# Half of the modulation vectors of a two-block network: from TensorE matmuls to VectorE multiply-and-sum, on one core

## What is computed

```python
for i in range(DEPTH):                      # two layers
    mod = silu(c) @ ada_w[i] + ada_b[i]     # c: 1024, ada_w[i]: 1024 x 6144
    sh1, sc1, g1, sh2, sc2, g2 = split(mod, 6)
    mod_c = silu(c_ctx) @ ada_w[i] + ada_b[i]   # the same for the context
    h = rmsnorm(x) * (1 + sc1) + sh1        # and hc of ctx by mod_c
    y, yc = attention(h, hc) if i == 0 else ssm(h, hc)
    x = x + g1 * y
    x = x + g2 * swiglu(rmsnorm(x) * (1 + sc2) + sh2)
    ...                                     # ctx likewise, in layer 0
```

## Time and profile before

| | |
|---|---|
| time, median of 3 runs (lowest, highest) | 1482.14 us (1481.31, 1489.8) |
| the profiled execution: time, span | 1486.74 us, 1484.9 us |
| TensorE busy | 1441.1 us, 97% of the span |
| VectorE busy | 801.4 us, 54% |
| ScalarE busy | 628.9 us, 42% |
| GpSimd busy | 295.3 us, 20% |
| moved from and to device memory | 206.81 MB, mean 139 GB/s |
| mean granted TensorE clock | 0.988 |

### The profile page before, as it was taken

One profiled execution on the slowest core, in us unless ns is written; L12 is line 12 of the kernel. 1 busy time (PEld: TensorE's weight loads), 2 busy tenths in 40 slices (PEclk: granted clock), 3 DMA queues, 4 the chain that ended last, 5 costly groups with the idle time before them and its releaser, 6 DMA issues. The chain is left out here.

```text
span 1484.9 us, 22118 instructions
## 1 busy us (share of the span) xinstructions
PE 1441.1 (97%) x9039; PEld 1202.4 (81%) x9050; DVE 801.4 (54%) x1341; ACT 628.9 (42%) x1183; POOL 295.3 (20%) x217
## 2 busy tenths in 40 slices
PE   7999999999989999999999999999999999999997
PEld 6978888888755778888888887888998778888886
DVE  6775645465299363233222324864543876476674
ACT  4536444653378343221122223442443574364452
POOL 2002355350000012110021110444500121021121
PEclk9999999999999999999999999999999999999999
DMA  7643688553100252223232333232451253656551
GB/s 229 216 146 113 233 319 324 190 194 150 57 1 1 75 209 85 85 89 134 76 112 69 100 110 119 86 113 85 142 179 49 103 182 140 258 181 215 177 175 48
DMA packets 36124, 206.81 MB, mean 139 GB/s; under 512 B 4968, under 2 KB 9496, under 8 KB 14904
## 3 DMA queue, kind: packets, MB, share of 16 engines
q1 hardware_dynamic: 32832, 199.58, 37.3%
q10 hardware_dynamic: 2376, 3.04, 1.1%
q0 software_dynamic: 816, 2.78, 0.6%
HBM read 202.76 MB, written 2.62 MB: 138 GB/s over the span
## 5 line engine op out<-in xcount | busy, mean ns | idle before, releaser
L645 DVE TENSOR_TENSOR w_split<-ring,w_split 128x1024 fp32r<-128x1024 f32 (+1 forms) x140 | 193.0, 1381 | 326.3 <-ACT w_split L640 325.7
L640 ACT ACTIVATE w_split<-ring 128x1024 fp32r<-128x1024 f32 (+1 forms) x140 | 157.9, 1133 | 369.6 <-PE lin L2085 259.2
L2083 PE MATMUL lin<-hn_hi,w_split 128*128 128x512 f32 x440 | 172.8, 393 | 0.0
L2085 PE MATMUL lin<-hn_hi,w_split 128*128 128x512 f32 x440 | 171.3, 389 | 0.0
L2084 PE MATMUL lin<-hn_lo,w_split 128*128 128x512 f32 x400 | 155.7, 389 | 0.0
L2115 PE MATMUL lin<-hn_hi,w_split 128*128 128x512 f32 x328 | 114.0, 394 | 0.0
L587 POOL TENSOR_TENSOR hn<-hn 128x256 f32<-128x256 f32 (+1 forms) x36 | 44.4, 1234 | 334.7 <-ACT hn L737 334.3
L604 POOL CAST hid_split<-arena 128x512 fp32r<-128x512 f32 (+1 forms) x44 | 26.0, 592 | 407.0 <-DVE arena L1167 269.7
L2083 PEld LDWEIGHTS lin<-hn_hi,w_split 128*128 128x128 f32 x440 | 82.6, 188 | 18.2 <-issue 1.3
L2085 PEld LDWEIGHTS lin<-hn_hi,w_split 128*128 128x128 f32 x440 | 82.6, 188 | 17.4
L645 POOL TENSOR_TENSOR w_split_od<-ring,w_split_od 128x1024 fp32r<-128x1024 f32 x31 | 75.7, 2455 | 81.7 <-ACT w_split_od L640 81.6
(11 more groups left out here) (517 smaller groups left out, 3481.0 us busy)
## 6 DMA issues: line engine op xcount, KB each, us to landing
ring<-ada_in SPq DMA_DIRECT2D x48, 1024.0 KB, 5.1
ring<-ssm_in_in SPq DMA_DIRECT2D x24, 1024.0 KB, 4.8
ring<-od_in_in SPq DMA_DIRECT2D x12, 1024.0 KB, 5.3
ring<-ffn0a_in_in SPq DMA_DIRECT2D x11, 1024.0 KB, 4.8
ring<-ffn0b_in_in SPq DMA_DIRECT2D x11, 1024.0 KB, 4.8
ring<-ffn1a_in_in SPq DMA_DIRECT2D x11, 1024.0 KB, 4.9
ring<-ffn1b_in_in SPq DMA_DIRECT2D x11, 1024.0 KB, 4.8
ring<-ev_in_in SPq DMA_DIRECT2D x9, 1024.0 KB, 13.4
```

Source lines behind the costliest of these rows:

```text
L640: act.activation(parts[:, 0], w, ACT.Copy).then_inc(sig("w_high"), 1)
L645: dve.tensor_tensor(parts[:, 1], w, parts[:, 0].bitcast(F32), ALU.subtract).then_inc(sig("w_low"), 1)
L2083: mm(lin[0:m, tile % RING, 0:width], hi, x_hi, start=kt == 0, stop=False)
L2085: ins = mm(lin[0:m, tile % RING, 0:width], lo, x_hi, start=False, stop=kt == kts - 1)
```

## The change

24 of the 48 modulation blocks stay with TensorE (output tiles 0 to 39 and 88 to 95, groups 0 to 4 and a last one that is now number 5). The other 48 output tiles (40 to 87) are laid out the other way round, outputs on the partitions and the 1024 inputs along the row (`ada_rows`, 24 blocks of 1 MB, two tiles in each). VectorE multiplies such a tile with a row vector that stands on all partitions and sums along the row in the same instruction (`accum_out`), once for c and once for c_ctx: four instructions of 128 x 1024 a block, 96 in all, two after each of the units 4 to 51 (of 60) of the first feed forward. The row vectors come by a new load of 1 MB on GpSimd's queue (`c_rows`), which waits until the last tile of `w_o` has been read, and ScalarE applies silu to them (128 x 2048). `STREAM` carries the row blocks between the weights of the first feed forward.

```diff
-    *[(name, n, 2 * KT * P) for _ in range(6) for name, n in (("od_in", 1), ("ada", 2))],
-    *[(name, 1, 2 * KT * P) for _ in range(3) for name in ("od_in", "ada")], ("ada", 1, 2 * KT * P),
-    ("od_out", 4, 2 * KT * P),
+    *[(name, n, 2 * KT * P) for _ in range(4) for name, n in (("od_in", 1), ("ada", 2))],
+    ("od_in", 5, 2 * KT * P), ("od_out", 4, 2 * KT * P),
...
-    ("ada", 2, 2 * KT * P), ("ffn0a_in", 2, 2 * KT * P), ("ada", 2, 2 * KT * P), ("ffn0a_in", FH - 2, 2 * KT * P),
-    ("ffn0a_out", KT, FH * P), ("ffn0b_in", FH, 2 * KT * P), ("ffn0b_out", KT, FH * P),
+    ("ada", 2, 2 * KT * P), ("ffn0a_in", 4, 2 * KT * P),
+    *[(name, 1, 2 * KT * P) for _ in range(7) for name in ("ada_rows", "ffn0a_in")],
+    *[part for _ in range(4) for part in (("ada_rows", 1, 2 * KT * P), ("ffn0a_out", 2, FH * P))],
+    *[(name, 1, 2 * KT * P) for _ in range(11) for name in ("ada_rows", "ffn0b_in")],
+    *[part for _ in range(2) for part in (("ada_rows", 1, 2 * KT * P), ("ffn0b_out", 2, FH * P))], ("ffn0b_out", 4, FH * P),
...
+            taken(pool, "lin", lin_of["w_o"] + KT - 1)
+            pool.dma_start(c_rows, t["c_rows"].unsqueeze(0).to_broadcast([P, 2, D])).then_inc(sig("c_rows_in"), 16)
             sum_squares(pool, own, 3, 2 * L)
...
+            act.wait_ge(sig("c_rows_in"), 16)
+            act.activation(c_rows, c_rows, ACT.Silu).then_inc(sig("silu_rows"), 1)
             ffn_scalar(act, 0, 2 * L)
...
-            for stage, u, later in ffn_units(n):
+            for v, (stage, u, later) in enumerate(ffn_units(n)):
                 tile = lin_of[stage] + u
                 if later is not None:
                     weights_lo(dve, *later)
-                if stage[-4:] == "a_in" and u == 8:
-                    modulations(dve, own, group, 1)
+                if n == 0 and 4 <= v < 4 + 2 * ROW_BLOCKS:
+                    modulation_rows(dve, own, v - 4)
...
+        def modulation_rows(dve, own, m):
+
+            r, j = divmod(m, 2)
+            b, n = blocks_of["ada_rows"][r], ROW_TILES + m
+            if m == 0:
+                dve.wait_ge(sig("silu_rows"), 1)
+            if j == 0:
+                dve.wait_ge(w_in[b % RING], 16 * (b // RING + 1))
+            for s in range(2):
+                ins = dve.scalar_tensor_tensor(
+                    out=row_products, in0=ring[:, b % RING, j * D:(j + 1) * D], scalar=1.0, in1=c_rows[:, s],
+                    op0=ALU.mult, op1=ALU.mult, accum_out=mod_tiles[:, n, s:s + 1])
+                own.link(ins)
+            if j == 1:
+                dve.sem_inc(sig("ada_rows_used"), 1)
+            if m in (7, 2 * ROW_BLOCKS - 1):
+                tiles = slice(ROW_TILES if m == 7 else ROW_TILES + 8, n + 1)
+                own.link(dve.tensor_tensor(mod_tiles[:, tiles], mod_tiles[:, tiles], each(mod_bias[:, tiles], 2), ALU.add))
...
-                if 3 <= u_ < 16 or u_ == 17 or 20 <= u_ < 23:
+                if 3 <= u_ < 12:
                     ada(1)
...
-                if 5 <= n < 7:
-                    ada(1)
...
             for i in range(DT_ + 2):
-                if i in (5, 12, 16):
-                    ada_groups((5, 12, 16).index(i) + 8)
                 if i == DT_:
                     y_sums(0)
-                if i < 2 or 5 <= i < 9 or 12 <= i < 16:
-                    ada(1)
...
-                if 5 <= n < 7:
-                    ada(1)
```

More of the change, by code:

```diff
@@ L379, in program @@
         silu_g = mem.take(2, 2 * L)
+        row_products = mem.take(D)
+        c_rows = mem.take(2, D)
         mem = Memory(arena)
@@ L847, in od_weights @@
                     weights_hi(act, "qkv", m)
-            act_norm(act, 2, 2 * L, "od_out", (0, 0, 0), before=od_weights, later=6)
+            act_norm(act, 2, 2 * L, "od_out", (0, 0, 0), before=od_weights, later=4)
             def exps(i, j):
@@ L915, in first_weights @@
                 weights_hi(act, "ssm_in", 1)
-            act_norm(act, 4, 2 * L, "ffn0b_out", (1, 0, 2), first_weights, between=lambda: weights_hi(act, "ssm_in", 2))
+            act_norm(act, 4, 2 * L, "ffn0b_out", (1, 0, 2), first_weights, between=lambda: weights_hi(act, "ssm_in", 2),
+                     later=5)
             weights_hi(act, "ssm_in", 3)
@@ L1021, in next_weights @@
                         weights_hi(act, "ffn1a_in", m)
-            act_norm(act, 5, L, "ssm_out", (1, 3, 3), before=next_weights, later=11)
+            act_norm(act, 5, L, "ssm_out", (1, 3, 3), before=next_weights)
             ffn_scalar(act, 1, L)
@@ L2003, in _ @@
             q1_low(KT - 1)
-            modulations(dve, own, 0, 6)
+            modulations(dve, own, 0, 4)
             def query_weights(n):
@@ L2656, in feed_forward @@
                         split_linear(stage + "_in", KT, lambda kt: (hn_hi[:, kt, :], hn_lo[:, kt, :]), width,
-                                     later=later, norm=start)
+                                     norm=start)
                         split_linear(stage + "_out", FH, lambda kt: (hid_split[:, 0, kt, :], hid_split[:, 1, kt, :]),
@@ L2891, in layout @@
                           for n in range(2)])
-    o["ada"] = ada
+    o["ada"] = np.concatenate([ada[:20], ada[44:]])
+    rows = np.stack([i["ada_w_2"][n].T.reshape(48, P, D) for n in range(2)]).reshape(96, P, D)
+    rows = rows[ROW_TILES:ROW_TILES + 2 * ROW_BLOCKS].reshape(ROW_BLOCKS, 2, P, D)
+    o["ada_rows"] = rows.transpose(0, 2, 1, 3).reshape(ROW_BLOCKS, P, 2 * D)
+    o["c_rows"] = np.stack([i["c_2"][0], i["c_ctx_2"]])
     o["gcol"] = columns(i["norm_g"])
```

59 lines of the change are left out of this document (31 added, 28 removed).

## The result

The changed kernel takes 1489.57 us (median of 20 runs, 1486.17 to 1492.86), the kernel before 1486.83 in the 20 runs beside it (1481.31 to 1489.8): a ratio of 1.0027, 95% interval [1.0017, 1.0037]. By this interval the change costs 2.5 to 5.5 us where 2.7 us of gain were forecast. The forecast of 1480 was tied to the 1482.14 of the three runs shown then; the larger set puts the kernel before 4.7 us higher, so 4.7 of the 9.6 us between 1480 and 1489.6 are this reference, and the rest is the error of the prediction. The kernel before varies with its clock: of 11 runs on one chip five took 1481.5 to 1482.9 us at a mean granted clock of 0.991, the other six 1487.0 to 1488.3 at 0.988. By the profiled executions the span grew from 1484.9 to 1490.1 us, and the mean granted clock fell from 0.988 to 0.977.

A forecast was written before the change was run, and what follows sets the result against it. TensorE was taken as the bound. 25.0 saved - 10.0 seams - 8.1 norm - 4.2 clock = 2.7 us faster than the profiled 1486.74, so 1484.0, or 1479.5 by the runs' median; predicted 1480, range 1466 to 1500.

The forecast's parts named there:

- TensorE's clock: Half-speed stretches behind new pauses: 1.7 us at each of two seams, 0.8 at the norm behind w_o, together 4.2 lost.
- the two blocks at the norm that follows fill waits of TensorE: nothing: At the norm behind ssm_out, taking out two blocks that fill TensorE's waits was to save nothing.
- TensorE saves 25.0 us: Blocks and groups removed: od_in 9.0, w_o 2.5, loop over heads 10.6, ssm_out 2.3, feed forwards 0.6 us.
- the wait for VectorE's shares: In the attention behind od_in, TensorE arrives earlier without the blocks and waits 1.7 us for VectorE.
- Row sum 1.3 us: Time of one summing VectorE instruction in the first feed forward; 96 of them 125 us, VectorE keeping pace up to 1.95 each.
- Seams 10.0 us: Between in- and out-product, TensorE waits for VectorE's last product: 4.9 and 5.1 us, bounds 3.4 and 16.
- the ring's lateness: At a seam, the third out-block loads only after unit 19's row sums, landing at 668.8, 4.3 us late.
- Norm behind `w_o` 8.1 us: The c_rows load ahead of GpSimd's six sums of squares makes TensorE wait 8.1 us longer, range 7.5 to 9.
- Rival A: First feed forward: VectorE becomes the pace from 1.95 us a row sum; at 2.3 us about 1523 us; chance 0.13.
- Rival B: Seams cost little, with the ring never late and the clock staying: 1469 to about 1466 us; chance 0.15.
- Rival C: ScalarE and VectorE pace the loop over heads, its 10.6 us saving shrinks to some 4: 1486 us; chance 0.12.

The follow-up runs named there:

- e3_both: Changed kernel with the c_rows load issued behind GpSimd's sums of squares and the row sums around the seams moved into out-units: 1464.50 us, ratio 0.9873 to before.
- e2_seam: Changed kernel with no row sums around the seams, their eight tiles' sums moved into the first half's out-units: 1477.33 us, ratio 0.9952 to before.
- e1_norm: Changed kernel with the c_rows load issued behind, not ahead of, GpSimd's sums of squares at the norm behind w_o: 1478.56 us, ratio 0.9957 to before.
- e6b_fill: Changed kernel with useless matmuls in TensorE's new pauses, 37 at the norm behind w_o and 16 at either seam: 1482.89 us, ratio 0.9984 to before.
- e10_load: Kernel before with only the c_rows load added ahead of GpSimd's sums of squares, all blocks staying with TensorE: 1493.90 us, ratio 1.0061 to before.
- e5_fill5: Changed kernel with load and seam row sums moved, plus ten useless matmuls at each of two places at the norm behind ssm_out: 1465.00 us, ratio 0.9871 to before.
- e4_none: Changed kernel without the row-block and c_rows loads, the silu and the 96 row sums: 1466.61 us, ratio 0.9873 to before.
- e7_path: Changed kernel without the row sums of units 18, 19, 48 and 49: 1481.39 us, ratio 0.9977 to before.
- e8_twice: Changed kernel with every row sum done twice, one behind the other: 1575.46 us, ratio 1.0605 to before.

## Why the prediction was wrong, step by step

The step that failed is **"TensorE's clock": "I count 1.7 for each of the two new pauses at the seams ... the longer pause may add 0.8. Together 4.2, bounds 0.8 and 6."** The mechanism was right, the size was not. I had taken the price of a pause from one place, the 1.88 us at 304.28 with its 3 us at 0.50, and used it for pauses of 4.6 and 9.7. Even for its own length that was one case of several: this pause is the same in all 14 executions (1.86 to 1.88 us), and 3.4 us at 0.50 follow it in five, 6.8 in two, none in seven. Windows behind it in the changed kernel, e3_both and e2_seam:

```profile
297.60:300.50 2.90, 2.90 (x14) 2.90 (x15) 0.79 (x3) 1.18 (x2) 0.04 (x1) 0.50 0.71 246
293.90:299.80 5.90, 5.90 (x27) 5.90 (x28) 0.81 (x3) 1.58 (x2) 2.39 (x1) 0.50 0.49 181
296.50:300.50 4.00, 4.00 (x33) 4.00 (x34) 0.89 (x4) 1.68 (x3) 1.81 (x1) 1.00 0.76 266
```

And at the norm behind `w_o` the kernel before is at 0.50 from 547.2 to 550.6; the 2.2 us of the earlier trace rows are only the part of it that was read.

Measured, the out-products are 7.5 and 7.9 us longer with pauses of 4.59 and 4.76, so 6.05 for the clock at the seams (3.4 predicted; 4.1 in e1_norm); filling the pauses gave 4.7 of these back with the hold left nearly as it was (e6b_fill). At the norm behind `w_o` it is 2.0 (0.8 predicted; e10_load has it alone). And one more place was counted at nothing: "the two blocks at the norm that follows fill waits of TensorE: nothing" is true of the waits, but without them the stretch at 0.50 behind that norm doubled from 3.4 to 6.8 us in the changed kernel, and fills there took it away (e5_fill5, in the trace alone). It costs 1.0: the second feed forward is 0.4 longer, though it lost a group of 0.6. Together some 9.1 against 4.2 and beyond the bound of 6: these 4.9 us are more than the 2.7 of the forecast, and turn its sign. The figure is that of the profiled executions; in a run of the median time it is some 2 us lower.

The Trainium skill (TensorE: Matmul & The Clock Gate, under Terms) puts the penalty at the throttled time by one less the ratio, here half of it. For the seams that gives 3.4 each by the stretch of 6.8; measured are 3.0, since TensorE was still waiting in a part of it. The halving was not what I missed, it was the length.

Point by point:

- **TensorE saves 25.0 us.** About 23.1: `od_in` 8.2 (9.0 predicted; the wait for VectorE's shares 1.55, 1.7 predicted), `w_o` 2.5 (2.5), loop over heads 10.2 (10.6), `ssm_out` 1.6 (2.3), groups 0.6 (0.6). The trace of e4_none agrees; its 18.9 us by time are this saving less what the clock took back. A second, smaller error, 1.9 us.
- **Row sum 1.3 us.** Right: 1.244 in the mean, one every 1.26 with the read-out (656.70 to 657.95 and 661.44 to 662.70 in the trace). The Trainium skill's halving (Vector Engine (DVE) Microarchitecture Reference, under Points that are easy to get wrong) is not borne out for this form, by which one would have taken some 2.3.
- **Seams 10.0 us.** Right: 9.35, by the very chain that was written down. The third out-block is issued at 664.02 at the end of unit 19's sums, has landed when ScalarE starts on it at 668.08 (668.8 predicted), the product comes at 677.82 and TensorE goes on at 680.58 (681.4 predicted). e7_path leaves 1.79 and 2.00 without the ring's lateness (1.7 predicted).
- **Norm behind `w_o` 8.1 us.** 9.0: the order is as predicted, but six sums take 8.85 and not 8.1, since one of them ran beside VectorE's work and took 2.13 us. The top of the range of 7.5 to 9 is just what came.
- **Rival A** did not come about; e8_twice shows its mechanism at twice the size; where between the two it sets in was not tried. **Rival B**, seams that cost little: no, they cost 15.4 us with the clock. **Rival C**, a loop over heads paced by others: no, 10.2 of 10.6 came.

The measured terms give 23.1 - 9.35 - 9.0 - 9.1 = -4.35, so 4.3 us slower; the profiled executions differ by 5.2. The rest lies at places that are not in this sum: 1.3 slower ahead of the norm behind `ev_out`, 1.4 faster in the attention, 0.8 slower behind the norm of `ffn0b_out` (6.8 us at 0.50 in place of 3.4) and 0.4 at the end. Stretches at 0.50 come and go also where no edit reaches: ahead of the norm behind `ev_out`, where all executions run the same code, they sum to between 0 and 6.8 us, and the stage lasts 170.6 to 174.5 us; in the attention the changed kernel had one fewer than the kernel before.

## What to carry to other kernels

Price a new pause of TensorE at its length plus the work behind it at half speed, and take the stretch from pauses of similar length, in more than one execution: here 4.6 to 4.9 us of waiting cost 6.2 to 7.9. Before work is handed to an idle engine, look at what the handing over puts into other queues: one DMA issue ahead of six sums cost 11 us here, and sixteen of 96 row sums beside a seam another 15, while the other eighty cost next to nothing; moving both turned +0.3% into -1.3%, and two smaller touches made it -1.7%. And small work that fills an engine's waits is not free to remove when that engine's clock hangs on its being busy.

## What the runs showed of the hardware that I had not expected

- The same pause is not always followed by the same clock: 4.57 us at the first seam of e1_norm by 3.4 us at 0.50, 4.59 in the changed kernel by 6.8; 1.79 in e7_path by none, 2.00 by 3.4; the 1.88 in `od_out` by none, 3.4 or 6.8. Useless matmuls in a pause are a real speed-up (e6b_fill, 6.4 us).
- The last feed forward runs at one of two paces, at a place where the programs are alike and with a clock of 1.00: 925 matmuls in 160 us (before, after, e3_both) or 907 (e5_fill5; 908 in e2_seam), some 3.5 us over the stage. The out-product there takes 30.5 us in seven of the 14 executions and 31.1 in the other seven. No experiment tells why.
- GpSimd and VectorE can slow each other down where they work at the same time: GpSimd's addition of two 128x512 tiles took 2.13 us beside VectorE and 1.26 alone, VectorE's product of 128x16 1.23 us beside it and 0.17 elsewhere. It came out the same in e10_load (2.13), so it is the place and not chance. At the norm behind `od_out` the same additions take 1.60 to 2.04 us beside VectorE in the kernel before too, so the price stood in the trace that the prediction was made from.
